# Forgetting attention: VectorE normalises the preceding unit's rows ahead of the maximum of this slot's scores

## The chip, the cores and the metric

The kernel runs on one core of one Trainium2 chip. The core has a matrix engine (TensorE, PE in the rows below, with its weight loads as PEld), VectorE (DVE), ScalarE (ACT), GpSimd (POOL), and SyncE (SP), which here only starts DMAs. Each engine takes its instructions strictly in its own program order, and they meet only at semaphores. The metric is device time in microseconds (us) of one execution.

## The reference

The reference is a trunk of two layers over a stream of 512 tokens of width 1024, in float32. Layer 0 has a mixer of a gated recurrence and differential attention, layer 1 has forgetting attention; each is followed by a residual LayerNorm and by a SwiGLU block (2816 wide) with another LayerNorm. The part that matters here is the attention of layer 1, with 16 heads of width 64:

```python
s = einsum('bhqd,bhkd->bhqk', qb, k) * scale + (cb[..., :, None] - c[..., None, :])
mask = k_pos[None, :] <= q_pos[:, None]
p = jax.nn.softmax(jnp.where(mask, s, MASK_VALUE), axis=-1)
return jnp.einsum('bhqk,bhkd->bhqd', p, v)
```

q and k are projections of the stream, each head's row scaled by the inverse root of its mean square; c is the running sum of the log forget gates. The output is multiplied with sigmoid(g) and goes through an output projection.

## The kernel before

**Products.** Every large product is split in three (high by low, low by high, high by high halves of float32), so TensorE carries three matmuls for each one of the reference. The weights come in 107 chunks through a ring: DMA to `w_raw`, ScalarE rounds to `w_hi` (L1036, 1.9 us for a whole chunk), GpSimd takes the rest to `w_lo` (L996, four instructions in a row), TensorE consumes.

**Slots.** In layer 1 the projections and the attention are interleaved by one list, `fox_steps`, which every engine walks. A step has a quarter of a weight chunk (a "piece") or a "slot" number s, or both. There are 32 units of attention, each a pair of heads (8) by a tile of 128 queries (4); unit u has keys 0 to (u mod 4 + 1) x 128, so its tiles are 128, 256, 384 and 512 wide in turn. In slot s

- TensorE does the piece, then turns a finished tile of q or k (`turn_heads`, L849, to bank 3), then the scores of unit s (L863 to L871, two banks out of 5, 6, 7), then transposes the probabilities of unit s-2 (`turn_pair`, L879, banks 3 and 4), then multiplies those of unit s-3 with v (L897, bank 2);
- ScalarE, after the work on the piece of the step before, takes the two exponentials of unit s with their row sums (L1286), then copies one transposed map of unit s-2 (L1229);
- VectorE, after the work on the pieces before, takes the row maxima of unit s (in one instruction, L1621, where its banks lie side by side, else in two, L1624 and L1625), normalises the maps of unit s-1 (a reciprocal, L1632, and two multiplications, L1635), copies the other transposed map of unit s-2 (L1644), and evacuates an output of unit s-3 where one is due.

**The path of q and k.** A piece of q or k goes round the engines: ScalarE copies it to `q_raw` and squares it to `sq` (L1058, L1254); VectorE sums the squares and adds epsilon (L1566, L1567); ScalarE takes logarithm and exponential (L1053, L1054); VectorE refines the root (L1332 to L1335) and scales the rows (L1577, `qn`); TensorE turns them into bank 3; ScalarE copies them to `qk` (L1263). Bank 3 is also the first bank of `turn_pair`, so TensorE's L879 waits for that copy. These pieces lie at the slots 0 to 4, 8 to 12 and 16 to 20; elsewhere the pieces are of v or of the gate and need none of this.

**Waits around the change.** `chain(ins, sem)` lets the engine go on only when the instruction is done. `full(key)` waits for a bank that TensorE has filled. `fmax` (VectorE to ScalarE) releases the exponentials, `fexp` (ScalarE to VectorE) says that unit u's exponentials are done, `fnorm` (VectorE to TensorE) releases `turn_pair`. The maximum of slot s >= 4 already waits for `fexp` of unit s-4; the normalisation of unit s-1 waits for `fexp` of unit s-1.

Of the kernel before, what the change touches and what calls it, by code (L numbers as in the profile page):

```python
# [35 lines left out]
ALU = mybir.AluOpType  # L36
# [3 lines left out]
P = 128  # L40
D = 1024
TS = 512
NT = TS // P
# [83 lines left out]
def build(nc, w, out):  # L127
# [5 lines left out]
    with ExitStack() as ctx:  # L133
# [6 lines left out]
        def place(name, free, dt, size):  # L140
            t = at(name, [P, *free], dt, top[0])
            n = size
            for f in free:
                n *= f
            top[0] += -(-n // 32) * 32
            return t
# [15 lines left out]
        small = place("small", [48], F32, 4)  # L162
# [4 lines left out]
        def take(name, free, dt, at_el):  # L167
            t = at(name, [P, *free], dt, arena + 4 * at_el)
            n = 1
            for f in free:  # L170
                n *= f
            return t, at_el + n
# [40 lines left out]
        p_fox, e = take("p_fox", [3, 2, TS], F32, e)  # L213
# [16 lines left out]
        def sem(name):  # L230
            return ctx.enter_context(nc.semaphore(name))
# [10 lines left out]
        act_step, dve_step = sem("act_step"), sem("dve_step")  # L242
        T_hi, T_lo = sem("T_hi"), sem("T_lo")
        S = {}
# [73 lines left out]
        n = 0  # L318
# [23 lines left out]
        F_UNITS = PAIRS * NT  # L342
# [12 lines left out]
        def heads_at(i):  # L355

            if not 0 <= i < len(fox_steps) or fox_steps[i][0] is None:
                return None
            c, p = fox_steps[i][0]
            stage = chunks[c][0]  # L360
            if stage[3] not in "qk":
                return None
            part, j = "qk".index(stage[3]), int(stage[4])
            return part, j, p, (2 * j + part) * NT + p
# [635 lines left out]
        def reader_of(eng, counts):  # L1000
            def full(key):
                bank, n, _ = uses[key]
                eng.wait_ge(bank_full[bank], n)
                return psum[bank]

            def chain(ins, s):

                ins.then_inc(s, 1)
                counts[id(s)] = counts.get(id(s), 0) + 1
                eng.wait_ge(s, counts[id(s)])  # L1010

            return full, chain
# [291 lines left out]
        def _(dve):  # L1304
            counts = {}
            full, chain = reader_of(dve, counts)
            step = lambda ins: chain(ins, dve_step)
            release = lambda ins, key: chain(ins, freed["dve"][uses[key][0]])
            v = nc.vector
            tt, ts, stt = v.tensor_tensor, v.tensor_scalar, v.scalar_tensor_tensor  # L1310
# [151 lines left out]
            for s in range(N + 4 + ROOT_LAG):  # L1462
# [3 lines left out]
                u = s - 4  # L1466
# [8 lines left out]
                if s < N:  # L1475
                    n = (s % NT + 1) * P
# [4 lines left out]
                    c, b = 24 + 4 * (s % 2), uses[("score", s, 0)][0]  # L1481
                    chain(v.tensor_reduce(small[:, c:c + 2], banks[:, b:b + 2, 0:n], AX_X, ALU.max, negate=True),  # L1482
                          S["max_done"])
                if 1 <= s <= N:

                    u = s - 1
                    n = (u % NT + 1) * P
                    c = 26 + 4 * (u % 2)
# [6 lines left out]
                u = s - 4 - ROOT_LAG  # L1495
# [67 lines left out]
            def square_sums(part, j, t, n):  # L1563
                dve.wait_ge(S["sq_done"], n + 1)
                m = fox_ms[:, n % 2, :, :]
                step(v.tensor_reduce(m[:, 0, :], sq[:, n % 2, :].rearrange("p (h d) -> p h d", h=4), AX_X, ALU.add))  # L1566
                chain(ts(m[:, 0, :], m[:, 0, :], 1.0 / HD, 1e-6, ALU.mult, ALU.add), S["qvar"])  # L1567

            def fox_heads(part, j, t, n):

                m = fox_ms[:, n % 2, :, :]
                dve.wait_ge(S["qroot"], n + 1)
                refine(m[:, 1, :], m[:, 0, :], m[:, 2, :])
                if n >= 2:

                    full(("heads", n - 2))
                chain(tt(qn[:, n % 2, :].rearrange("p (h d) -> p h d", h=4),  # L1577
                         q_raw[:, n % 2, :].rearrange("p (h d) -> p h d", h=4),
                         m[:, 1, :].unsqueeze(2).to_broadcast([P, 4, HD]), ALU.mult), S["qn_done"])
# [13 lines left out]
            for i, (piece, s) in enumerate(fox_steps):  # L1593
                if i == 2:
                    z, e = gate_T[0:FH, 0, :], gate_T[0:FH, 1, :]
                    release(ts(z, full("fox_f")[0:FH, :], gains[0:FH, 6:7], None, ALU.add), "fox_f")
                    chain(stt(e, z, -1.0, z, ALU.mult, ALU.min), S["f_arg"])
                    step(ts(z, z, 0.0, None, ALU.min))
                    dve.wait_ge(S["f_ln"], 1)
                    step(v.tensor_tensor_scan(z, z, e, 0.0, ALU.add, ALU.subtract))  # L1600

                    parts = [c_parts[0:FH, k, :] for k in range(3)]
                    step(ts(parts[0], z, -1.0, None, ALU.mult))
                    step(stt(z, z, -1.0, parts[0], ALU.mult, ALU.subtract))
                    step(v.tensor_copy(parts[1], z))
                    step(tt(z, z, parts[1], ALU.subtract))
                    chain(v.tensor_copy(parts[2], z), S["c_split"])
                if heads_at(i - 2):
                    fox_heads(*heads_at(i - 2))
                if heads_at(i - 1):  # L1610
                    square_sums(*heads_at(i - 1))
                if s is not None and s < F_UNITS:
                    n = (s % NT + 1) * P
                    c = 2 * (s % 4)
                    if s >= 4:
                        dve.wait_ge(S["fexp"], s - 3)
                    for m in range(2):
                        full(("fs", s, m))
                    a, b = SCORE_BANKS[s % 3]
                    if b - a == 1:  # L1620
                        ins = v.tensor_reduce(small[:, 16 + c:18 + c], banks[:, a:b + 1, 0:n], AX_X, ALU.max,  # L1621
                                              negate=True)
                    else:
                        step(v.tensor_reduce(small[:, 16 + c:17 + c], psum[a][:, 0:n], AX_X, ALU.max, negate=True))  # L1624
                        ins = v.tensor_reduce(small[:, 17 + c:18 + c], psum[b][:, 0:n], AX_X, ALU.max, negate=True)  # L1625
                    chain(ins, S["fmax"])
                if s is not None and 1 <= s <= F_UNITS:

                    u = s - 1
                    n, c = (u % NT + 1) * P, 2 * (u % 4)  # L1630
                    dve.wait_ge(S["fexp"], u + 1)
                    step(v.reciprocal(small[:, 32 + c:34 + c], small[:, 24 + c:26 + c]))  # L1632
                    for m in range(2):
                        p = p_fox[:, u % 3, m, 0:n]
                        ins = ts(p, p, small[:, 32 + c + m:33 + c + m], None, ALU.mult)  # L1635
                        chain(ins, S["fnorm"] if m else dve_step)
                if s is not None and 2 <= s < F_UNITS + 2:

                    u = s - 2
                    n = (u % NT + 1) * P  # L1640
                    acc = full(("fT", u, 1))
                    if u >= 2:
                        full(("fv", u - 2))
                    release(v.tensor_copy(pT_fox[:, u % 2, 1, 0:n], acc[:, 0:n]), ("fT", u, 1))  # L1644
                    dve.sem_inc(S["fpT_b"], 1)
                if s is not None and s >= 3:
                    u = s - 3
                    pair, t = u // NT, u % NT
                    acc = full(("fv", u))
                    if pair == PAIRS - 1:  # L1650
                        tok = slice(t * P, (t + 1) * P)
                        release(out_gate(pair, acc[:, tok], tok), ("fv", u))
                        dve.sem_inc(S["o_gated"], 1)
                        if t == 0:
                            out_lo(4)
                            out_lo(5)
                            out_lo(PAIRS - 2)
                        out_lo(pair, tok, t)
                    elif t == NT - 1 and pair == PAIRS - 2:
                        release(out_gate(pair, acc[:, :]), ("fv", u))  # L1660
                        dve.sem_inc(S["o_gated"], 1)
                    elif t == NT - 1:
                        release(v.tensor_copy(oT[:, pair, :], acc[:, :]), ("fv", u))
                f = gate_at(i - 1)
                if f is not None and f <= 5:
                    chain(out_gate(f, oT[:, f, :]), S["o_gated"])
                if f == 2:
                    out_lo(0)
                if f is not None and 2 <= f <= 4:
                    out_lo(f - 1)  # L1670
# [57 lines left out]
```

## Time and profile before

| | us |
|---|---|
| median of 3 runs (lowest, highest) | 1447.54 (1446.81, 1448.47) |
| the profiled execution's own time | 1443.57 |
| its span, first to last instruction | 1441.4 |
| TensorE busy in the span | 1363.5 (95%) |
| VectorE, ScalarE, GpSimd busy | 504.0, 492.8, 528.6 |
| mean granted TensorE clock | 0.981 |

The layer's attention, slots 0 to 31, lies between 774 us and 1030 us of the span. A row of the timeline has the start in us from the span's start, the duration in us, engine, line, operation, what is written and read, and in square brackets how long the engine had been idle before it and what ended that.

### The profile page before, as it was taken

The page shows a single profiled execution, that of the slowest core. Times are in us where ns is not written, and L with a number is a line of the kernel's source. Part 1 is how long each engine was busy: PE and PEld are TensorE (multiplying, and loading weights), DVE is VectorE, ACT ScalarE, POOL GpSimd, SP SyncE. Part 2 cuts the span into 40 slices and gives each one's busy share as a digit, 9 for nine tenths or more (in the row PEclk, how much of TensorE's full clock was granted, in tenths as well). Part 3 has the DMA queues.
Part 4 walks back from the last instruction along what each step waited for, and adds up shares of the span by engine and source line. Part 5 has one row for each costly group of instructions (what it writes and reads, how often), then busy time and mean ns, then how long its engine had stood idle before and what let it go on. Part 6 is the DMA issues. An engine that isn't in the chain of part 4 may idle for free.

```text
span 1441.4 us, 19076 instructions
## 1 busy us (share of the span) xinstructions
PE 1363.5 (95%) x7304; PEld 1132.6 (79%) x7304; DVE 504.0 (35%) x1054; ACT 492.8 (34%) x830; POOL 528.6 (37%) x421
## 2 busy tenths in 40 slices
PE   7999997789999999999988999899999999999997
PEld 7888874568888888887877778767788888888876
DVE  3366435655111111011653565654471111110005
ACT  4312326433223223211354554554333232232120
POOL 5421322042544543643333221222234445445350
PEclk9999998899999999999989999999999999999999
DMA  6311121022233232333133112202122332333231
GB/s 222 100 52 59 59 88 30 30 88 60 88 110 95 88 103 88 102 102 104 60 88 88 52 39 59 59 30 85 63 88 88 97 108 88 92 99 117 74 116 59
DMA packets 140137, 119.56 MB, mean 83 GB/s; under 512 B 5600, under 2 KB 118416, under 8 KB 140048
## 3 DMA queue, kind: packets, MB, share of 16 engines
q1 hardware_dynamic: 140048, 118.36, 26.5%
q8 instruction: 58, 0.95, 0.3%
q14 instruction: 31, 0.25, 0.1%
HBM read 116.20 MB, written 2.10 MB: 82 GB/s over the span
## 4 chain that ended last, share of the span: by engine, by line
PE 78%; DVE 9%; ACT 6%; issue 4%; POOL 2%; DMA 0%; ACTq 0%; DVEq 0%; POOLq 0%; SPq 0%
PE banks L471 24%; PE banks L473 23%; PE banks L472 23%; ACT w_hi L1036 2%; POOL w_lo L996 2%; PE banks L750 1%; PE banks L863 1%; PE banks L897 1%; PE banks L879 1%; DVE fox_ms L1567 1%; PE banks L817 1%; PE banks L768 1%; DVE small L1482 1%; DVE fox_ms L1566 1%; DVE o_even L1448 1%
## 5 line engine op out<-in xcount | busy, mean ns | idle before, releaser
L996 POOL TENSOR_TENSOR w_lo<-w_raw,w_hi 128x512 fp32r<-128x512 f32 x417 | 528.4, 1300 | 876.6 <-ACT w_hi L1036 847.5
L471 PE MATMUL banks<-xT_lo,w_hi 128*128 128x512 f32 (+2 forms) x992 | 371.9, 375 | 2.6 <-DVEq L1328 2.6
L473 PE MATMUL banks<-xT_hi,w_hi 128*128 128x512 f32 (+2 forms) x992 | 368.7, 372 | 0.0
L472 PE MATMUL banks<-xT_hi,w_lo 128*128 128x512 f32 (+2 forms) x992 | 368.6, 372 | 0.0
L1036 ACT ACTIVATE w_hi<-w_raw 128x2048 fp32r<-128x2048 f32 (+1 forms) x107 | 200.0, 1870 | 186.2 <-PE banks L473 143.6
L471 PEld LDWEIGHTS banks<-xT_lo,w_hi 128*128 128x128 f32 (+1 forms) x992 | 186.4, 188 | 36.3 <-issue 4.9
L473 PEld LDWEIGHTS banks<-xT_hi,w_hi 128*128 128x128 f32 (+1 forms) x992 | 186.5, 188 | 32.6
L472 PEld LDWEIGHTS banks<-xT_hi,w_lo 128*128 128x128 f32 (+1 forms) x992 | 186.6, 188 | 31.5
L471 PE MATMUL banks<-w_lo,xT_hi 128*128 128x256 f32 (+1 forms) x544 | 187.8, 345 | 15.5 <-ACT q_raw L1058 10.0
L472 PE MATMUL banks<-w_hi,xT_lo 128*128 128x256 f32 (+1 forms) x544 | 181.5, 334 | 0.0
L473 PE MATMUL banks<-w_hi,xT_hi 128*128 128x256 f32 (+1 forms) x544 | 181.5, 334 | 0.0
L1546 DVE TENSOR_TENSOR banks<-silu_g,banks 128x512 f32<-128x512 f32 x44 | 30.6, 696 | 402.7 <-PE banks L473 402.7
L471 PE MATMUL banks<-w_lo,hT_hi 128*128 128x512 f32 x352 | 137.3, 390 | 3.6 <-POOL w_lo L996 3.6
L473 PE MATMUL banks<-w_hi,hT_hi 128*128 128x512 f32 x352 | 137.0, 389 | 0.0
L472 PE MATMUL banks<-w_hi,hT_lo 128*128 128x512 f32 x352 | 136.9, 389 | 0.0
L1201 ACT ACTIVATE silu_g<-banks 128x512 f32<-128x512 f32 x44 | 26.4, 599 | 306.9 <-PE banks L473 306.9
L471 PEld LDWEIGHTS banks<-w_lo,xT_hi 128*128 128x128 f32 x544 | 106.9, 197 | 29.9 <-ACT q_raw L1058 11.0
L473 PEld LDWEIGHTS banks<-w_hi,xT_hi 128*128 128x128 f32 x544 | 107.0, 197 | 9.2
L472 PEld LDWEIGHTS banks<-w_hi,xT_lo 128*128 128x128 f32 x544 | 107.2, 197 | 8.1
L1507 DVE SCALAR_TENSOR_TENSOR x_res<-x_res,banks 128x512 f32<-128x512 f32 x32 | 22.0, 688 | 219.5 <-PE banks L473 218.8
L471 PEld LDWEIGHTS banks<-w_lo,hT_hi 128*128 128x128 f32 x352 | 66.1, 188 | 18.0 <-issue 4.4
L473 PEld LDWEIGHTS banks<-w_hi,hT_hi 128*128 128x128 f32 x352 | 66.1, 188 | 13.8
(178 smaller groups left out, 1229.8 us busy)
## 6 DMA issues: line engine op xcount, KB each, us to landing
w_raw<-in_ffn_w_dram SPq DMA_DIRECT2D x92, 512.0 KB, 4.1
w_raw<-in_ffn_w_dram SPq DMA_DIRECT2D x20, 1024.0 KB, 5.0
w_raw<-in_fox_w_in_dram SPq DMA_DIRECT2D x16, 1024.0 KB, 5.9
w_raw<-in_even_w_in_dram SPq DMA_DIRECT2D x14, 1024.0 KB, 5.0
w_raw<-in_even_w_out_dram SPq DMA_DIRECT2D x4, 1024.0 KB, 5.0
w_raw<-in_fox_w_out_dram SPq DMA_DIRECT2D x4, 1024.0 KB, 4.9
x_res<-in_x_dram SPq DMA_DIRECT2D x4, 512.0 KB, 7.7
out_dram<-x_res SPq DMA_DIRECT2D x4, 512.0 KB, 2.6
```

Of the source, the lines that this page charges most:

```text
L471: mm(acc, l_hi, r_lo, start=first, stop=False)
L472: mm(acc, l_lo, r_hi, start=False, stop=False)
L473: return mm(acc, l_hi, r_hi, start=False, stop=final)
L750: ins = mm(halves(acc[:, tok], z)[:, :, 1, :], k[:, tok], halves(q[:, tok], z)[:, :, 1, :], start=True, stop=True)
L768: ins = mm(acc[:, t * P:(t + 1) * P], scT[:, h % 2, PAIR[(s, t)], :], iv[:, s, h * P:(h + 1) * P], start=s == 0, stop=s == t)
L817: mm(acc[:, 0:n], bqT[rows, h, i * P:(i + 1) * P], bkT[rows, h, 0:n], start=True, stop=False)
L863: mm(acc[:, 0:n], qk[rows, j % 2, 0, pair % 2, i * P:(i + 1) * P], qk[rows, j % 2, 1, pair % 2, 0:n], start=True, stop=False)
L996: ins = nc.gpsimd.tensor_tensor(w_lo[c % RING][:, a:a + n], w_raw[c % RAW][:, a:a + n], w_hi[c % RING][:, a:a + n].bitcast(F32), ALU.subtract)
L1036: chain(fn(w_hi[c % RING][:, 0:size], w_raw[c % RAW][:, 0:size], ACT.Copy), hi_ready)
L1201: release(fn(silu_buf(j), acc[:, :], ACT.Silu), (f"up{l}", j, 0))
L1507: release(stt(xs, xs, ALPHA, full(key)[:, :], ALU.mult, ALU.add), key)
L1546: release(tt(h_buf(j), silu_buf(j), acc[:, :], ALU.mult), (f"up{l}", j, 1))
```

## The change

On VectorE, and only there, the block that normalises unit s-1 (with its wait for `fexp`) is moved from behind the maximum of unit s to ahead of it. In the program after the change the normalisation is at L1612 to L1621 and the maximum at L1622 to L1636.

```diff
                 if heads_at(i - 1):
                     square_sums(*heads_at(i - 1))
+                if s is not None and 1 <= s <= F_UNITS:
+
+                    u = s - 1
+                    n, c = (u % NT + 1) * P, 2 * (u % 4)
+                    dve.wait_ge(S["fexp"], u + 1)
+                    step(v.reciprocal(small[:, 32 + c:34 + c], small[:, 24 + c:26 + c]))
+                    for m in range(2):
+                        p = p_fox[:, u % 3, m, 0:n]
+                        ins = ts(p, p, small[:, 32 + c + m:33 + c + m], None, ALU.mult)
+                        chain(ins, S["fnorm"] if m else dve_step)
                 if s is not None and s < F_UNITS:
                     n = (s % NT + 1) * P
                     c = 2 * (s % 4)
...
                     chain(ins, S["fmax"])
-                if s is not None and 1 <= s <= F_UNITS:
-
-                    u = s - 1
-                    n, c = (u % NT + 1) * P, 2 * (u % 4)
-                    dve.wait_ge(S["fexp"], u + 1)
-                    step(v.reciprocal(small[:, 32 + c:34 + c], small[:, 24 + c:26 + c]))
-                    for m in range(2):
-                        p = p_fox[:, u % 3, m, 0:n]
-                        ins = ts(p, p, small[:, 32 + c + m:33 + c + m], None, ALU.mult)
-                        chain(ins, S["fnorm"] if m else dve_step)
                 if s is not None and 2 <= s < F_UNITS + 2:
```

VectorE's rows at slot 3, before (`fox_ms` holds the sums and roots of q or k, `small` the maxima, row sums and reciprocals, `p_fox` the maps, `banks` PSUM):

```order
L1566 TENSOR_REDUCE fox_ms<-sq 128x4
L1567 TENSOR_SCALAR fox_ms<-fox_ms 128x4
L1621 TENSOR_REDUCE small<-banks 128x2
L1632 RECIPROCAL small<-small 128x2
L1635 TENSOR_SCALAR p_fox<-p_fox,small 128x384 x2
L1644 COPY pT_fox<-banks 128x256
L1332 TENSOR_TENSOR fox_ms<-fox_ms 128x4
```

VectorE's rows at the same place after the change:

```order
L1566 TENSOR_REDUCE fox_ms<-sq 128x4
L1567 TENSOR_SCALAR fox_ms<-fox_ms 128x4
L1617 RECIPROCAL small<-small 128x2
L1620 TENSOR_SCALAR p_fox<-p_fox,small 128x384 x2
L1631 TENSOR_REDUCE small<-banks 128x2
L1644 COPY pT_fox<-banks 128x256
```

The reciprocal and the two multiplications of unit 2 have passed the maximum of unit 3; what follows the three stays where it was. The same holds in slot 31, here as the difference, VectorE again:

```order
-L1624 TENSOR_REDUCE small<-banks 128x1
-L1625 TENSOR_REDUCE small<-banks 128x1
-L1632 RECIPROCAL small<-small 128x2
-L1635 TENSOR_SCALAR p_fox<-p_fox,small 128x384 x2
+L1617 RECIPROCAL small<-small 128x2
+L1620 TENSOR_SCALAR p_fox<-p_fox,small 128x384 x2
+L1634 TENSOR_REDUCE small<-banks 128x1
+L1635 TENSOR_REDUCE small<-banks 128x1
 L1644 COPY pT_fox<-banks 128x256
```

Nothing else moves on VectorE, and the order on TensorE, ScalarE, GpSimd and SyncE is the same in both programs.

## Rows read from the trace of the kernel before

**Rows 1.** Waits of TensorE in 773 to 1030 us: total, times, longest.
```profile
PE banks L879 <- ACT qk L1263: 10.4, 8, 2.3
```

**Rows 2.** Timeline of VectorE, slots 1 to 3.
```profile
784.53 0.42 DVE L1624 TENSOR_REDUCE small<-banks 128x1 f32<-128x256 f32 x1
...
785.45 0.17 DVE L1632 RECIPROCAL small<-small 128x2 f32<-128x2 f32 x1
785.65 0.61 DVE L1635 TENSOR_SCALAR p_fox<-p_fox,small 128x128 f32<-128x128 f32 x2
...
788.43 0.96 DVE L1621 TENSOR_REDUCE small<-banks 128x2 f32<-128x768 f32 x1
...
789.63 0.75 DVE L1635 TENSOR_SCALAR p_fox<-p_fox,small 128x256 f32<-128x256 f32 x2
...
798.88 1.23 DVE L1621 TENSOR_REDUCE small<-banks 128x2 f32<-128x1024 f32 x1
...
800.34 1.60 DVE L1635 TENSOR_SCALAR p_fox<-p_fox,small 128x384 f32<-128x384 f32 x2
...
803.87 0.42 DVE L1566 TENSOR_REDUCE fox_ms<-sq 128x4 f32<-128x256 f32 x1
```

**Rows 3.** Timeline of ScalarE, slots 2 and 3.
```profile
789.61 0.58 ACT L1286 ACTIVATE p_fox<-banks,small 128x384 f32<-128x384 f32 x1 [0.17 <-ACT qk L1263]
...
800.14 0.69 ACT L1286 ACTIVATE p_fox<-banks,small 128x512 f32<-128x512 f32 x1 [0.25 <-DVE small L1621]
...
802.82 0.42 ACT L1254 ACTIVATE sq<-q_raw 128x256 f32<-128x256 f32 x1
```

**Rows 4.** Timeline of TensorE, its waits in slots 3 and 4.
```profile
800.03 0.63 PE L879 MATMUL banks<-ident,p_fox 128*128 128x128 f32 x4 [2.26 <-ACT qk L1263]
...
805.69 0.85 PE L879 MATMUL banks<-ident,p_fox 128*128 128x128 f32 x6 [0.56 <-ACT qk L1263]
```

**Rows 5.** Timeline of GpSimd, two of its bursts.
```profile
796.34 4.93 POOL L996 TENSOR_TENSOR w_lo<-w_raw,w_hi 128x512 fp32r<-128x512 f32 x4 [13.37 <-ACT w_hi L1036]
...
858.73 4.93 POOL L996 TENSOR_TENSOR w_lo<-w_raw,w_hi 128x512 fp32r<-128x512 f32 x4 [14.80 <-PE banks L473]
```

**Rows 6.** Timeline of VectorE, slots 6, 8 to 11, 17 and 18.
```profile
822.22 2.52 DVE L1635 TENSOR_SCALAR p_fox<-p_fox,small 128x256 f32<-128x256 f32 x2
...
834.70 0.42 DVE L1621 TENSOR_REDUCE small<-banks 128x2 f32<-128x256 f32 x1 [1.68 <-PE banks L871]
...
845.50 0.69 DVE L1621 TENSOR_REDUCE small<-banks 128x2 f32<-128x512 f32 x1
...
850.24 0.56 DVE L1624 TENSOR_REDUCE small<-banks 128x1 f32<-128x384 f32 x1 [0.31 <-PE banks L871]
...
861.28 1.23 DVE L1621 TENSOR_REDUCE small<-banks 128x2 f32<-128x1024 f32 x1
...
909.05 0.69 DVE L1621 TENSOR_REDUCE small<-banks 128x2 f32<-128x512 f32 x1
...
917.27 0.96 DVE L1621 TENSOR_REDUCE small<-banks 128x2 f32<-128x768 f32 x1 [1.01 <-PE banks L871]
```

**Rows 7.** Timeline of ScalarE, slots 7, 11 and 19.
```profile
832.29 0.69 ACT L1286 ACTIVATE p_fox<-banks,small 128x512 f32<-128x512 f32 x1
...
868.31 0.47 ACT L1263 ACTIVATE qk<-banks,gains 128x256 f32<-128x256 f32 x1 [0.89 <-PE banks L849]
...
935.85 0.47 ACT L1263 ACTIVATE qk<-banks,gains 128x256 f32<-128x256 f32 x1 [1.16 <-PE banks L849]
```

**Rows 8.** Timeline of TensorE: slots 11 and 19, and the last unit.
```profile
862.43 0.63 PE L879 MATMUL banks<-ident,p_fox 128*128 128x128 f32 x4 [1.90 <-ACT qk L1263]
...
929.98 0.63 PE L879 MATMUL banks<-ident,p_fox 128*128 128x128 f32 x4 [1.96 <-ACT qk L1263]
...
1028.40 1.09 PE L897 MATMUL banks<-pT_fox,v_all 128*64 128x128 f32 x16 [0.75 <-DVE oT L1584]
```

**Rows 9.** Stages: us, busy times, granted clock, DMA share, GB/s.
```profile
930.00:935.00 5.00, 5.00 (x30) 4.66 (x31) 3.51 (x14) 3.16 (x9) 0.00 (x0) 0.67 0.46 153
```

## The prediction, made before the changed kernel was run

> **What bounds the kernel now.** I read the page first: TensorE is busy 95% of the span, so a change on VectorE can cost or bring only what it adds to or takes from TensorE's waits. The reader then looks at the waits of TensorE within the attention of layer 1. They are few: eight of its transposes of the probabilities (L879) wait 10.4 us in all for ScalarE's copy to `qk` [rows 1]. These waits lie where pieces of q and k go round the engines beside the slots: slots 1 to 4, 8 to 11, 16 to 20. In all other slots TensorE does not wait, and VectorE has time. Third, the timeline of VectorE, for one question in each slot: was the engine idle before the maximum? Seven times of 32 it was not: slots 1, 2, 3, 9, 11, 17 and 19. In slots 1 to 3 the scores lie ready and the maximum starts as soon as VectorE is free [rows 2]. Elsewhere it waited for the scores, for 0.31 us in slot 10, 1.01 in slot 18, 1.68 in slot 8 [rows 6] and mostly for longer.
>
> **What is moved and its size.** 32 normalisations are moved, of which 31 pass a maximum. Each is a reciprocal and two multiplications. The 128-wide one takes 0.84 us: 785.45 to 785.65 for the reciprocal, 0.61 for the pair, 0.03 for the hand-over. The 256-wide takes 0.20 + 0.75 + 0.04 = 0.99. The 384-wide took 0.20 + 1.60 + 0.04 = 1.84 in slot 3 [rows 2]. Undisturbed the widths suggest 1.12: between 128 and 256 columns the pair grew by 0.14, so 0.75 + 0.14 = 0.89, and 0.23 around it. For 512 the same step gives 1.25. Nothing is added or removed, and no DMA or queue is passed. The work on other engines stays in order, so only dates change.
>
> **Where VectorE was idle: nothing or a small gain.** With an idle time longer than the normalisation, it fits in ahead of the maximum and the maximum keeps its date. The copy behind it comes earlier by as much. TensorE does not wait for that copy or for `fnorm` in any slot (no such wait stands among those of rows 1), so the gain has no taker. One small taker may be at the end: the last product with v waited 0.75 us for VectorE's output step [rows 8]. That step follows the copy of the last unit's transposed map, which cannot start before TensorE has turned it, so I credit 0.1 to 0.2 of the 0.75.
>
> **Where VectorE was not idle: the maximum is late, and the exponentials, and all behind them on ScalarE.** Those are the q and k steps on which TensorE waits.
>
> Stretch one, slots 1 to 4. In slot 1 the maximum is 0.84 late. In slot 2 another 0.99 is put before it. Before, the exponentials of slot 2 did not start at the end of the maximum (788.43 + 0.96 = 789.39, some 0.09 to the other engine) but at 789.61, behind a `qk` copy [rows 3], so 0.13 is absorbed: 0.84 + 0.99 - 0.13 = 1.70. This goes through `q_raw`, `sq`, the sums, the root and the `qk` copy, at each of which the next engine was waiting, to the L879 at 800.03, where TensorE already waits [rows 4]: 1.70 us later. In slot 3 the 384-wide normalisation comes before the maximum. GpSimd's burst for the next chunk (796.34, four instructions in 4.93 us [rows 5]) moves with ScalarE's rounding, so by 1.70 too, to 798.0 to 803.0. The normalisation now starts at 798.88 + 1.70 = 800.6, at the same place in the burst at which the maximum used to stand, and no longer at its end. What a pair of multiplications costs inside a burst is in slot 6: 2.52 us for the 256-wide pair that took 0.75 otherwise [rows 2, 6], as if each multiplication had to wait for the instruction of GpSimd under way (4.93 / 4 = 1.23 us). Here the burst ends after 2.4 us, so I take 2.5 for the whole normalisation; bounds 1.12 (undisturbed) and 2.7. The exponentials of slot 3 are then 1.70 + 2.5 = 4.2 late. On the way to the next wait there is slack: `sq` was done at 802.82 + 0.42 = 803.24 [rows 3], VectorE summed it at 803.87 [rows 2], so 0.63 - 0.1 = 0.53 is absorbed. TensorE's L879 at 805.69 [rows 4] is 4.2 - 0.5 = **3.7 us** later (2.3 undisturbed, 3.9 at most). Behind it TensorE is busy without a wait until the next stretch, so nothing of it is given back.
>
> The Trainium skill (SBUF — State Buffer, section "Who interferes with whom") says that VectorE and GpSimd share one pair of ports as an exclusive lock, which an instruction holds to its end while the other is blocked. It speaks against this change: the maximum reads PSUM and is not subject to the lock, the multiplications on SBUF are, and the change lets them take the maximum's place within the burst. The trace agrees with it at 822.22 (2.52 us). By a sharing of bandwidth in its place the 384-wide normalisation would stay near the 1.84 us of its row, and stretch one would come to 3.0 us.
>
> Stretch two, slots 9 to 11. Slot 9: 0.84. Slot 10: 0.99 less the idle 0.31, so 1.5; about 0.45 goes into the slack before the sum as above, and the L879 at 862.43 is 1.1 later [rows 8]. Slot 11: the 384-wide normalisation again falls inside a burst (858.73 + 1.1 to 863.66 + 1.1; it starts at 861.28 + 1.1 = 862.4 [rows 5, 6]): 2.6, so 3.7 for the exponentials, less 0.45 of slack, less the 0.89 that the next `qk` copy had waited for TensorE [rows 7]. That leaves **2.3 us** (1.1 undisturbed).
>
> Stretch three, slots 17 to 20. Slot 17: 0.84, through to the L879 at 929.98 [rows 8]. Slot 18: the idle 1.01 takes the 0.99. Slot 19: 1.12 more, outside a burst, and the next `qk` copy had waited 1.16 for TensorE [rows 7], so it is absorbed. **0.8 us**.
>
> Sum: 3.7 + 2.3 + 0.8 - 0.1 = 6.7 us. Against the profiled execution's own 1443.57 that is 1450.3; the median of the runs is 1447.54, some 4 us above that execution, and I put the same 6.7 on it: **1454.2 us**.
>
> **The added wait.** The maximum of slot s now stands behind the exponentials of unit s-1. The tightest place is slot 8: those of slot 7 end at 832.29 + 0.69 and about 0.2 for the row sum, the 512-wide normalisation then needs 1.25 and ends at 834.4, the scores are ready for the maximum at 834.70 [rows 6, 7]. It fits by some 0.3 us. If it did not, slots 8, 16 and 24 would cost a few tenths each, under 1 us.
>
> **Rivals.**
> - Only part arrives. The bursts do not hit the moved multiplications (the undisturbed bounds: 2.3 + 1.1 + 0.8 - 0.1 = 4.1, so 1451.6). For it: the burst's phase is an argument of mine from 1.7 us of shift. Against it: 1.60 us in slot 3 was already disturbed.
> - Nearly nothing arrives. Only the first delay of each stretch counts, since later ones overlap with TensorE's own waits: 3 x 0.84 = 2.5, so 1450.0. For it: 95% busy TensorE and short queues. Against it: in slots 2 and 3 the waiting engine is each time the next on the path.
> - Clock. TensorE's granted clock was 0.67 in the 5 us behind the wait at 929.98 [rows 8, 9], that is at the lower of its two levels (1.2 GHz) for two thirds of them; this costs 0.33 x 5 = 1.65 us where TensorE is the bound. Longer waits could bring two more such stretches: 6.7 + 3.3, so 1457.5.
> - Faster. The mechanism is the earlier copy and the earlier q and k work behind the maximum, in the slots where VectorE idles. It decides if the sum L1566 there starts when VectorE comes free and not when `sq` is done. If each of four of the eight L879 waits [rows 1] became shorter by 0.99, this would give -4, so 1443.5. Against it: behind the idle slots VectorE again waits for `sq`, and at slots 1 to 3 it is never idle, where the order alone can win nothing.
> - That the change does not do what it says is excluded by the order of the instructions.
>
> **How the numbers follow.** Forecast 0.40, bursts missed 0.25, clock 0.12, nearly nothing 0.17, faster 0.06. What a measurement of this kernel can tell from no change is about 0.2%, 2.9 us, so 1444.6 to 1450.4 is "same". Slower: 0.40 + 0.25 + 0.12 = 0.77; same 0.17; faster 0.06. The range goes from 1448.5, below the "nearly nothing" case, to 1458.5, above the clock case. Left out are the faster case and the tails.
>
> **What would show it.** In the profile after: TensorE's waits for the `qk` copy in the attention grow from 10.4 to some 17 us; the maxima of slots 1, 2 and 3 start 0.84, 1.8 and 4.2 us later against the start of slot 0; the pair of 384-wide multiplications in slots 3 and 11 takes 2 us or more; the pair in slot 6, moved ahead of its burst, falls to 0.75; from slot 21 on, the distances are unchanged. Wrong: a maximum late by 4 us in slot 3 with L879 on its old date, or VectorE's idle time before the maxima giving way to a wait for the exponentials.

## The result, and the profile after

| | before | after |
|---|---|---|
| median of the runs compared (lowest, highest), 4 each | 1448.01 (1446.81, 1451.13) | 1459.20 (1458.21, 1460.39) |
| ratio, 95% interval | | 1.0074 (1.0056 to 1.0093) |
| the profiled execution: own time, span | 1443.57, 1441.4 | 1460.39, 1458.3 |
| mean granted clock in it | 0.981 | 0.972 |

The kernel became slower by 0.74%, which is 10.7 us of 1448 (the two medians are 11.2 apart). The direction was as forecast, the size was not: 1454.2 had been forecast, and 1459.2 lies 0.7 above the end of the range. The page after, busy times of the engines:

```profile
PE 1374.2 (94%) x7304; PEld 1141.0 (78%) x7304; DVE 502.6 (34%) x1054; ACT 492.8 (34%) x830; POOL 529.0 (36%) x421
```

VectorE, ScalarE and GpSimd are as busy as before to 1.4 us. Only TensorE, with the same instructions, is busy 10.7 us longer (1363.5 before). The two spans differ by 16.9 us. Of these 5.2 are there before slot 0 begins, where both programs are the same (in the traces below slot 0 begins anywhere between 773.7 and 781.6 us), 10.5 come between the scores of slot 0 and those of slot 31, and 1.1 after. So I compare the stage from slot 0 to slot 31: before, then after (span, busy times of the five engines, granted clock, DMA share, GB/s).

```profile
774.40:1017.90 243.50, 228.67 (x1682) 182.78 (x1680) 139.37 (x346) 127.02 (x308) 59.92 (x48) 0.99 0.18 53
```
```profile
779.60:1033.60 254.00, 234.09 (x1681) 187.00 (x1680) 138.99 (x349) 127.02 (x308) 60.17 (x48) 0.96 0.17 51
```

10.5 us = 5.4 of TensorE busy and 5.1 of TensorE idle (14.8 to 19.9). The busy part is clock: by the granted clock, not rounded, TensorE was at the lower of its two levels for 6.8 us of the stage before and for 20.5 us after (the rounded 0.99 and 0.96 give 2 x 0.01 x 243 = 4.9 and 2 x 0.04 x 254 = 20.3). The idle part by cause, TensorE's waits in 778 to 1045 us after (total, times, longest), to hold against [rows 1]:

```profile
PE banks L879 <- ACT qk L1263: 9.8, 8, 1.8
PE banks L879 <- DVE p_fox L1620: 2.0, 1, 2.0
PE banks L863 <- ACT p_fox L1286: 2.0, 1, 2.0
PE banks L849 <- DVE qn L1577: 1.9, 2, 0.9
PE banks L849 <- ACT pT_fox L1229: 1.0, 1, 1.0
```

The waits for `qk` did not grow to 17: 9.8, and 11.8 with the row named `p_fox` L1620. That row is a `qk` wait under another name: the matmul starts at 944.49, the `qk` copy before it ended at 944.34 and the multiplication at 944.42, and the wait is put down to the last. What is new is L849, the turning of q and k, which before waited only once for 0.2 us, and 0.9 more at L863. Two of its three waits in the timeline of TensorE:

```profile
812.80 0.41 PE L849 MATMUL banks<-ident,qn 128*128 128x128 f32 x2 [1.03 <-ACT pT_fox L1229]
...
859.10 0.41 PE L849 MATMUL banks<-ident,qn 128*128 128x128 f32 x2 [0.95 <-DVE qn L1577]
```

L849 writes bank 3. Bank 3 must be free of unit s-3's transposed map, which ScalarE copies out (L1229) behind the exponentials, and these are late. The copy that frees bank 3 for the second of the two rows, on ScalarE:

```profile
858.35 0.60 ACT L1229 ACTIVATE pT_fox<-banks 128x512 f32<-128x512 f32 x1 [0.17 <-ACT p_fox L1286]
```

858.35 + 0.60 = 858.95, and 0.15 later L849 starts. The two others of its three waits ended 0.15 behind such a copy too (812.65 to 812.80, 926.25 to 926.40), and so did the start in the trace of before (848.20 to 848.35, with 0.07 of idle time there). The profile names `qn`, but the `qn` that it means is the next tile's; the tile turned here lay ready since 854.70. The late work reached TensorE through this bank too, not only through `qk`.

VectorE after, slots 2 and 3, to hold against [rows 2]:

```profile
789.97 0.61 DVE L1620 TENSOR_SCALAR p_fox<-p_fox,small 128x128 f32<-128x128 f32 x2
790.61 0.42 DVE L1634 TENSOR_REDUCE small<-banks 128x1 f32<-128x256 f32 x1
...
795.49 0.96 DVE L1631 TENSOR_REDUCE small<-banks 128x2 f32<-128x768 f32 x1
...
804.89 0.42 DVE L1566 TENSOR_REDUCE fox_ms<-sq 128x4 f32<-128x256 f32 x1 [3.04 <-ACT sq L1254]
805.35 1.17 DVE L1567 TENSOR_SCALAR fox_ms<-fox_ms 128x4 f32<-128x4 f32 x1
806.55 0.17 DVE L1617 RECIPROCAL small<-small 128x2 f32<-128x2 f32 x1
806.75 2.52 DVE L1620 TENSOR_SCALAR p_fox<-p_fox,small 128x384 f32<-128x384 f32 x2
809.31 1.23 DVE L1631 TENSOR_REDUCE small<-banks 128x2 f32<-128x1024 f32 x1
```

Slot 0 begins 5.22 us later than before. Measured from it, the maxima of slots 1, 2 and 3 are late by 790.61 - 784.53 - 5.22 = 0.86, by 795.49 - 788.43 - 5.22 = 1.84 and by 809.31 - 798.88 - 5.22 = 5.21. The first two are the forecast 0.84 and 1.8. The third was forecast at 4.2. The pair inside GpSimd's burst took 2.52, as in slot 6 before, and again in slot 11 (873.61, 2.52). The burst in slot 3:

```profile
804.00 5.06 POOL L996 TENSOR_TENSOR w_lo<-w_raw,w_hi 128x512 fp32r<-128x512 f32 x4 [15.81 <-ACT w_hi L1036]
```

The 5.21 divide into 2.44 by which L1566 is late (804.89 - 797.23 - 5.22; forecast 1.70) and 2.77 by which the maximum stands further behind it (4.42 us in place of 1.65; forecast 2.5). The 0.74 too much in the first goes with the clock: at 795 to 800 us TensorE was at its lower level, a stretch that the kernel before did not have, and in e6 below, without it, the shift at slot 3 is 4.42 = 1.65 + 2.77. Two of these windows after, in the first and third stretch of waits (columns as above):

```profile
795.00:800.00 5.00, 4.34 (x21) 4.37 (x22) 3.34 (x11) 2.91 (x9) 0.00 (x0) 0.50 0.00 0
945.00:950.00 5.00, 5.00 (x25) 4.34 (x24) 2.93 (x10) 2.87 (x8) 0.00 (x0) 0.50 0.36 123
```

The pair of slot 6 is ahead of its burst and fell to 0.74, and the tight place at slot 8 fitted: the maximum still waited 0.27 us for the scores, where 0.3 had been worked out.

```profile
827.79 0.74 DVE L1620 TENSOR_SCALAR p_fox<-p_fox,small 128x256 f32<-128x256 f32 x2
...
843.29 1.01 DVE L1620 TENSOR_SCALAR p_fox<-p_fox,small 128x512 f32<-128x512 f32 x2
844.57 0.42 DVE L1631 TENSOR_REDUCE small<-banks 128x2 f32<-128x256 f32 x1 [0.27 <-PE banks L871]
```

### The profile page after: what moved, and what is told of

It reads as the page before. It is cut to its first block, busy times and chain, and to the rows that moved or that the text cites. A ratio compares the mean times of both kernels' runs of the same rounds, so it can differ in the third digit from the quotient of the medians.

```text
span 1458.3 us, 19076 instructions
## 1 busy us (share of the span) xinstructions
PE 1374.2 (94%) x7304; PEld 1141.0 (78%) x7304; DVE 502.6 (34%) x1054; ACT 492.8 (34%) x830; POOL 529.0 (36%) x421
## 4 chain that ended last, share of the span: by engine, by line
PE 78%; DVE 9%; ACT 6%; issue 4%; POOL 2%; DMA 0%; ACTq 0%; DVEq 0%; POOLq 0%; SPq 0%
PE banks L471 24%; PE banks L473 23%; PE banks L472 23%; POOL w_lo L996 2%; ACT w_hi L1036 2%; PE banks L750 1%; PE banks L897 1%; PE banks L879 1%; PE banks L863 1%; DVE fox_ms L1567 1%; DVE fox_ms L1566 1%; DVE small L1482 1%; PE banks L768 1%; DVE p_fox L1620 1%; PE banks L817 1%
## 5 line engine op out<-in xcount | busy, mean ns | idle before, releaser
L471 PE MATMUL banks<-xT_lo,w_hi 128*128 128x512 f32 (+2 forms) x992 | 372.2, 375 | 2.0 <-DVEq L1328 1.6
L471 PEld LDWEIGHTS banks<-xT_lo,w_hi 128*128 128x128 f32 (+1 forms) x992 | 186.8, 188 | 35.9 <-issue 4.5
L471 PE MATMUL banks<-w_lo,xT_hi 128*128 128x256 f32 (+1 forms) x544 | 189.9, 349 | 15.2 <-ACT q_raw L1058 10.1
L471 PE MATMUL banks<-w_lo,hT_hi 128*128 128x512 f32 x352 | 138.7, 394 | 3.6 <-POOL w_lo L996 3.6
L471 PEld LDWEIGHTS banks<-w_lo,xT_hi 128*128 128x128 f32 x544 | 108.8, 200 | 30.1 <-ACT q_raw L1058 11.0
L471 PEld LDWEIGHTS banks<-w_lo,hT_hi 128*128 128x128 f32 x352 | 66.8, 190 | 18.2 <-issue 4.4
L472 PEld LDWEIGHTS banks<-w_hi,hT_lo 128*128 128x128 f32 x352 | 67.0, 190 | 13.9
```

Of the source, the lines that this page charges most:

```text
L471: mm(acc, l_hi, r_lo, start=first, stop=False)
L472: mm(acc, l_lo, r_hi, start=False, stop=False)
```

## The experiments

The measure within a trace is the shift: how much later than in the trace of before the maximum of a slot starts, both counted from the maximum of slot 0. It leaves out what happens before the attention. All are from one profiled execution each. The ratio compares whole runs, at least 6 of each kernel but for the 4 of the kernel after; 0.0010 of it is 1.4 us. It differs from the difference of the two medians by up to 1.5 us (e1).

| kernel | slot 1 | 2 | 3 | 5 | 8 | 13 | 16 | 31 | ratio to before (95%) |
|---|---|---|---|---|---|---|---|---|---|
| after | 0.86 | 1.84 | 5.21 | 4.67 | 4.65 | 8.36 | 8.36 | 10.53 | 1.0074 (1.0056, 1.0093) |
| e1, idle slots only | 0.01 | 0.02 | 0.02 | 0.84 | 0.84 | 0.01 | 0.01 | 0.07 | 1.0003 (0.9992, 1.0015) |
| e2, nine busy slots only | 0.86 | 1.84 | 4.59 | 5.53 | 5.52 | 8.08 | 8.08 | 8.93 | 1.0077 (1.0061, 1.0093) |
| e3, slots 1 to 3 only | 0.86 | 1.84 | 4.89 | 5.86 | 5.85 | 5.86 | 5.86 | 4.73 | 1.0049 (1.0032, 1.0067) |
| e4, slots 3 and 11 only | 0.02 | 0.02 | 2.78 | 2.25 | 2.25 | 3.70 | 3.69 | 3.68 | 1.0026 (1.0014, 1.0039) |
| e5, before, bank 4 first | 0.00 | 0.00 | 0.00 | -0.39 | -0.39 | -0.73 | -0.86 | -2.39 | 0.9967 (0.9955, 0.9978) |
| e6, after, bank 4 first, filled | 0.86 | 1.83 | 4.42 | 3.48 | 3.49 | 5.65 | 5.52 | 5.98 | 1.0033 (1.0017, 1.0048) |
| e7, before, bank 4 first, filled | 0.00 | 0.00 | 0.02 | -0.38 | -0.38 | -1.60 | -1.74 | -3.31 | 0.9973 (0.9960, 0.9985) |
| e8, e4 and fine bursts | -0.02 | -0.03 | 1.43 | 0.90 | 0.88 | 0.13 | 0.10 | 1.14 | 0.9989 (0.9973, 1.0005) |
| e9, before, fine bursts | -0.03 | -0.03 | 0.20 | 0.23 | 0.23 | -1.05 | -1.06 | -1.20 | 0.9977 (0.9966, 0.9988) |
| e10, before, bank 4 first, fine | -0.03 | -0.03 | 0.26 | -0.10 | -0.10 | -2.02 | -2.15 | -2.90 | 0.9954 (0.9940, 0.9969) |
| e11, after, fine bursts | 0.82 | 1.80 | 3.43 | 4.37 | 4.36 | 6.18 | 6.16 | 8.09 | 1.0030 (1.0016, 1.0045) |
| e12, after, bank 4 first | 0.84 | 1.81 | 4.40 | 3.45 | 3.46 | 6.45 | 6.32 | 6.83 | 1.0039 (1.0023, 1.0054) |

### Where the loss arises: idle slots against busy slots

**e1.** The order after, except in the nine slots of the three stretches; `normalise` is the moved block.

```diff
+                early = s not in (1, 2, 3, 9, 10, 11, 17, 18, 19)
+                if early and s is not None and 1 <= s <= F_UNITS:
+                    normalise(s)
...
+                if not early and s is not None and 1 <= s <= F_UNITS:
+                    normalise(s)
```

> The normalisation goes ahead of the maximum only in the 22 slots (and behind the last) in which VectorE had idled before the maximum; slots 1 to 3, 9 to 11 and 17 to 19 keep the old order. Theory 'late maxima' (the cost arises only where VectorE had no idle time, because the exponentials and with them the q and k work come late): no change, 0 to -0.5 us against the kernel before. Rival 'added wait' (each moved normalisation costs a little, because the maximum now stands behind the exponentials of the unit before): 23 of 32 moves kept, so about +8 of the +11 us.

Measured: 1446.98 against 1448.10, ratio 1.0003. Moving 22 of the 31 costs and brings nothing that the time of whole runs can show. The added wait for the exponentials costs nothing.

**e2.** The complement.

```diff
+                early = s in (1, 2, 3, 9, 10, 11, 17, 18, 19)
```

> The other way round: the new order only in slots 1 to 3, 9 to 11 and 17 to 19. Theory 'late maxima': the whole loss, +10 to +11.5 us against the kernel before. Rival 'added wait': 9 of 32 moves, about +3 us.

Measured: 1458.72, ratio 1.0077, the whole loss. Nine of 31 moves carry it, seven of them in slots without idle time; slots 10 and 18 had 0.31 and 1.01 us.

**e3.** The first stretch alone.

```diff
+                early = s in (1, 2, 3)
```

> The new order only in slots 1, 2 and 3. 'Late maxima' by the order alone: +3.7 us; the changed kernel's trace has +4.65 from slot 0 to slot 5, the difference being one low-clock stretch in slots 2 and 3, so with the clock +4.5 to +5. Rival 'nothing is given in part' (each stretch is absorbed by TensorE's next wait for q and k, and only all together cost): under +1.5 us.

Measured: 1454.25, ratio 1.0049, 7.1 us (the medians are 6.2 apart), more than the 4.5 to 5 that I had expected. The shift is 4.89 at slot 3 and 5.86 at slot 5. The last step, 0.97 where e4 falls by 0.53, comes with a low-clock stretch between slots 4 and 5, where TensorE does not wait. At slot 31 the shift is 4.73, since the low-clock stretch that before had from 931.7 on is missing. So slots 1 to 3 give roughly half or more of the loss.

### The pair of multiplications inside a burst

**e4.** Only the two slots in which the 384-wide normalisation takes the maximum's place within a burst.

```diff
+                early = s in (3, 11)
```

> The new order only in slots 3 and 11, where the 384-wide normalisation falls into a burst of GpSimd. If each multiplication waits for the instruction of GpSimd under way: pair of 2.2 to 2.5 us, exponentials 2.7 late, +2.1 in slot 3 and about +1.3 in slot 11, +3.4 us in all, with a low-clock stretch more +5. If the multiplications only share bandwidth (pair of about 1.6 us as before): 1.84 late less 0.5 of slack in slot 3 and nothing in slot 11 because the copy to qk had waited 0.9 for TensorE, so +1.3 to +1.8 us.

Measured: 1451.61, ratio 1.0026, 3.8 us (the medians are 3.5 apart), as expected; slot 5 late by 2.25, and 1.45 more at slot 13. VectorE in slot 3:

```profile
806.16 0.17 DVE L1618 RECIPROCAL small<-small 128x2 f32<-128x2 f32 x1
806.36 2.52 DVE L1621 TENSOR_SCALAR p_fox<-p_fox,small 128x384 f32<-128x384 f32 x2
```

**e8.** As e4, and GpSimd's instructions for the layer's input projections half as long and twice as many. If each multiplication waits for the instruction under way, the pair gets shorter; if the two share bandwidth, the same bytes cost the same.

```diff
-                for a in range(0, size, 512):
-                    n = min(512, size - a)
+                w = 256 if chunks[c][0].startswith("fox") else 512
+                for a in range(0, size, w):
+                    n = min(w, size - a)
```

> The new order only in slots 3 and 11, and GpSimd's instructions for the weights of this layer's input projection are 256 columns wide instead of 512, so each is about half as long and a burst has eight. If a multiplication of VectorE waits for GpSimd's instruction under way: the pair in slots 3 and 11 falls from 2.52 us to 1.3 to 1.8, and the loss of 3.7 us of the same order with 512-wide instructions falls to +1.5 to +2.5. If the two share bandwidth: pair at 2.5 us as before, loss unchanged.

Measured: 1447.90, ratio 0.9989: no loss is left, where 1.5 to 2.5 had been expected, since the fine bursts bring something by themselves (e9). The same pair, the burst that it falls into, and GpSimd's groups (busy us, mean ns):

```profile
801.66 1.36 DVE L1622 TENSOR_SCALAR p_fox<-p_fox,small 128x384 f32<-128x384 f32 x2
```
```profile
799.90 5.79 POOL L997 TENSOR_TENSOR w_lo<-w_raw,w_hi 128x256 fp32r<-128x256 f32 x8 [13.62 <-ACT w_hi L1037]
```
```profile
L997 POOL TENSOR_TENSOR w_lo<-w_raw,w_hi 128x512 fp32r<-128x512 f32 x352 | 447.4, 1303 | 659.1 <-ACT w_hi L1037 659.1
L997 POOL TENSOR_TENSOR w_lo<-w_raw,w_hi 128x256 fp32r<-128x256 f32 x128 | 90.6, 745 | 210.2 <-ACT w_hi L1037 182.3 <-PE banks L473 27.9
```

2.52 became 1.36 in both slots (864.07 too), while GpSimd's work on the same bytes got longer (2 x 745 ns in place of 1303). Outside a burst the 384-wide pair takes 0.88 (slot 19 of the kernel after, 943.54), so 1.64 of waiting became 0.48. The wait goes with the length of the neighbour's instruction, not with its bytes. The Trainium skill (SBUF — State Buffer, "Who interferes with whom") calls this an exclusive lock held to an instruction's end; this pair of traces agrees.

**e9.** The kernel before with that edit alone.

> The kernel before with GpSimd's instructions for this layer's input projection 256 columns wide. VectorE's instructions that waited 1.2 us inside a burst (among them the small ones at L1567 and L1332) should wait half as long; some of these lie on the q and k path: -1 to -3 us against the kernel before. If the fine instructions cost more (GpSimd 0.75 us each instead of half of 1.30, a burst 0.9 us longer) and a chunk comes late: 0 to +1.

Measured: 1443.36 against 1447.30, ratio 0.9977, a little more than expected. Against it, e8's order costs 0.67 at slot 5 (0.90 - 0.23) in place of 2.25: most of the price of slot 3 was the lock.

**e11.** The kernel after with it.

> The changed kernel with fine bursts. With the new order only in slots 3 and 11 the fine bursts took 2.5 us by the stage and 3.7 by the medians. The same in the full change: +6.5 to +8.5 us against the kernel before in place of +11. If the collision with the bursts did not matter in the full change: +10 to +11.

Measured: 1451.17, ratio 1.0030, so 8.0 us under the kernel after, and less than the 6.5 to 8.5 above the kernel before that I had expected. But e9 gained from the same edit, and against e9's 1443.36 the order still costs 7.8: fine bursts take away part of the price (2.9 of 10.7), not its root. In the traces it is less: the shift at slot 31 is 8.09 + 1.20 = 9.3 against e9, in place of 10.5.

### Clock and bank

**e5.** The kernel before, in which `turn_pair` turns the map of bank 4 first, so that the wait for bank 3 stands behind useful work.

```diff
-                for m in range(2):
+                for m in (1, 0):
...
-                        full(("fT", s - 3, 1))
+                        full(("fT", s - 3, 0))
```

> The kernel before, but TensorE transposes the map of the second head (bank 4) ahead of that of the first (bank 3), so that less of its work stands behind the wait for the copy to qk. The three stretches are latency chains through ScalarE and VectorE, so only the last wait of each stretch should shrink, by the 0.3 to 0.8 us of the transposes moved ahead: -0.5 to -2 us against the kernel before. If the waits add up one by one on TensorE instead: eight times 0.2 to 0.8, -3 to -4 us.

Measured: 1444.22 against 1448.83, ratio 0.9967. More in the median than I expected; in the trace 2.4, of which 1.8 arise in slots 19 to 20, where the low-clock stretch of before is missing.

**e6.** The kernel after with the same edit, and the first transposes repeated where TensorE would wait, so that it keeps working (the repeats write the same values).

```diff
+                    again = (6, 6, 2, 1)[u % NT] if m and u in (0, 1, 2, 8, 9, 10, 16, 17, 18) else 1
+                    for j in list(range(u % NT + 1)) * again:
```

> The changed kernel with bank 4 first, and in the slots of the q and k work the transposes into bank 4 are repeated (6, 6 or 2 times for 128, 256 or 384 keys; the same values are written again), so that TensorE works through much of its waits. Theory 'late maxima plus clock': the order costs about 7 of the 11 us and the rest is low granted clock called forth by the longer waits; with the waits filled the low-clock time between slots 0 and 31 falls from 20 us to under 7 and the kernel is at +5 to +7.5 us against the kernel before (the gain of bank 4 first is in that). Rival 'all is order': the clock changes or not, the time stays at +9 to +11.

Measured: 1452.59, ratio 1.0033, 4.8 us. That is just under the 5 to 7.5 of the theory, but it doesn't show that the order costs only 7: bank 4 first brought 4.8 us by itself in e5, more than I had taken for it. What the order costs follows from e7 below.

**e7.** The kernel before with both edits.

> The kernel before with the same two edits. Theory: bank 4 first brings 0.5 to 2 us and the filled waits up to the 3 us that its two low-clock stretches cost, so -1 to -4 us against the kernel before. If the fillers only lengthen TensorE's work where it does not wait long enough: 0 to +2 us.

Measured: 1444.91, ratio 0.9973. **e12**, the kernel after with bank 4 first and no repeats:

> The changed kernel with bank 4 first and no repeated transposes: the control of the run with filled waits (+3.3 per mille, +4.8 us). If the fillers did their part through the clock, this one lies between it and the changed kernel: +6 to +9 us, with a mean clock of 0.972 to 0.977 where the filled one has 0.981 to 0.984. If bank 4 first alone did it: +4.5 to +5.5 with the same clock as the filled one.

Measured: 1452.67 against 1447.30, ratio 1.0039, 5.6 us, with a mean clock of 0.977: the clock as I had expected it without the repeats, the time nearly that of e6. In the profiled executions of e6 and e7 the stage has no low-clock time at all:

```profile
776.30:1025.80 249.50, 232.48 (x1736) 185.34 (x1734) 139.23 (x349) 126.91 (x308) 60.11 (x48) 1.00 0.17 52
```
```profile
777.60:1017.90 240.30, 231.66 (x1736) 185.28 (x1734) 139.84 (x346) 126.88 (x308) 59.95 (x48) 1.00 0.18 54
```

So the difference of these two is the order alone, in kernels that both have bank 4 first and the repeats. It is 5.98 + 3.31 = **9.3 us** at slot 31: 3.86 by slot 5, 3.4 between 8 and 13 (2.16 against -1.22), 2.0 between 16 and 31 (0.46 against -1.57). e12 less e5 gives 9.2. Whole runs give 9.0 as the difference of the means of all 12 runs of e6 and e7, 7.7 as that of the medians. Where the clock is the same they agree better: runs of e6 with a mean clock of 0.983 or 0.984 took 1450.67 (mean of 4), those of e7 1441.64 (mean of 4), 9.0 apart; before and after at 0.974 to 0.976 took 1449.5 (10 runs) and 1459.1 (2 runs), 9.6 apart. The rest of the 10.7, some 1 to 2 us, is left for the clock: 0.974 in the mean of the runs after, 0.978 of before. It is a remainder and was not measured by itself.

Against a larger part of the clock speak e6 and e12: the repeats raised the mean clock from 0.977 to 0.981, and the time stayed (1.0033 and 1.0039, intervals overlap). The repeats take TensorE's time too, so this does not exclude a small part. In e1 to e4 the number and the place of the low-clock stretches differ from execution to execution, so one trace can't say how many the order brings.

**e10.** The kernel before with bank 4 first and fine bursts.

> The kernel before with bank 4 first and fine bursts. If the two gains are independent, the gain of bank 4 first (0.33%, 4.7 us) and that of the fine bursts (1 to 3 us) add: -5.5 to -7.5 us. If both mostly ease the same granted clock, they overlap: -4 to -5 us.

Measured: 1440.87 against 1447.30, ratio 0.9954: the best version, 6.4 us under the kernel before. That lies in the first branch: by the ratios it is 6.7, where the two edits alone give 4.8 and 3.3.

## Why the prediction was wrong in size

**Where it costs: right.** Only the three stretches in which VectorE had no or little idle time before the maximum count (e1 nothing, e2 all). "Faster" and "nearly nothing" fall with that, and so does a price of the added wait.

**Stretch one, 3.7: right.** 3.86 without low-clock time. The dates of slots 1 and 2 were met to 0.04, and the whole normalisation in the burst cost 2.77 where 2.5 (at most 2.7) had been taken. "Only part arrives" falls: the bursts did hit both pairs.

**Stretch two, 2.3, and stretch three, 0.8: the step that failed.** They measured 3.4 and 2.0. I had subtracted 0.89 and 1.16 because the next `qk` copy had waited that long for TensorE [rows 7], and took these waits for slack. They were made by the clock of that one execution. Before the first of them TensorE was at its lower level for two thirds of 5 us, and so it was before the second [rows 9]:

```profile
863.00:868.00 5.00, 5.00 (x31) 4.80 (x30) 3.40 (x10) 2.69 (x9) 0.67 (x1) 0.66 0.62 179
```

TensorE came late to L849, and ScalarE waited. In e7 the clock stays up at both places, and the two copies (slots 11 and 19) have no wait:

```profile
870.33 0.47 ACT L1264 ACTIVATE qk<-banks,gains 128x256 f32<-128x256 f32 x1
...
936.21 0.47 ACT L1264 ACTIVATE qk<-banks,gains 128x256 f32<-128x256 f32 x1
```

e7 has two more edits. e1 has none that touches these slots, and its trace says the same. There TensorE was at its lower level in slot 3, not in slot 11, and again in slot 19; the copies of slots 3, 11 and 19:

```profile
807.38 0.47 ACT L1263 ACTIVATE qk<-banks,gains 128x256 f32<-128x256 f32 x1 [0.85 <-PE banks L849]
...
869.78 0.47 ACT L1263 ACTIVATE qk<-banks,gains 128x256 f32<-128x256 f32 x1
...
937.38 0.47 ACT L1263 ACTIVATE qk<-banks,gains 128x256 f32<-128x256 f32 x1 [1.12 <-PE banks L849]
```

Without the two subtractions my own steps give 3.7 - 0.5 = 3.2 and 0.84 + 1.12 = 2.0, and with 3.7 and -0.1 a sum of 8.8, so 1456.3. What is missing from there to the 10.7 is 0.5 of sizes and the 1 to 2 us left for the clock. Where both executions have low clock at these places, the subtraction does hold: e2, TensorE at its lower level near both, has 2.56 in stretch two and 0.85 in stretch three against the trace of before, close to my 2.3 and 0.8. But in that trace stretch one cost 5.53 in place of 3.86, with low clock in slots 2 and 4, and the sum was 8.9 all the same. So I had counted what the low clock gives (waits that absorb a delay) and not what it takes. I had used [rows 9] to price a rival and had not asked what the same low clock did to the rows beside it.

**Clock, priced at nothing in the forecast: too low.** The lower level went from 6.8 to 20.5 us of the profiled stage, and TensorE was busy 5.4 longer. Most of that lay beside work that was late anyway: of the 10.5 us only 1.2 remain above the 9.3 of the order. The rival (two more stretches, +3.3) had the direction; in the runs 1 to 2 are left for it. What makes a stretch come in one execution and not in the next stays open.

**Where TensorE waits: half right.** I had named `qk` as the only channel (17 us), although the trace of before has waits of 1.1 at L863 and 2.8 at L471 in the attention too (2.8 after). Bank 3, freed by a ScalarE copy behind the late exponentials, is another: 2.9 us at L849, and 0.9 more at L863, while `qk` took 11.8 in place of 10.4.

**The small gain at the end, 0.1: right.** TensorE's wait for `oT` lies behind the maximum of slot 31, so the shifts don't show it. It is 0.75 us before and 0.63 after, and it follows the order of the last slots in the other traces too: 0.63 in e1, 0.74 to 0.75 in e2, e3 and e4, 0.58 in e7 against 0.48 in e6. The size is as forecast, the times of whole runs can't show it.

## What to carry to other kernels

Before moving a producer ahead of another on a shared engine, find in each slot whether that engine was idle there. Where it was not, the move delays the other producer by its full length (0.84 and 0.98 in slots 1 and 2), however rarely that is; where no one waits for its result, it brings nothing. A wait that you mean to subtract as slack must be there in other executions too; look at the granted clock just before it, since a low-clock stretch of the upstream engine makes such waits. Put those instructions of VectorE that a burst of GpSimd delays (here multiplications on SBUF) outside the bursts, or make the burst's instructions shorter; and let a consumer with two banks begin with the one that isn't awaited.

## What the runs showed of the hardware

A burst also delays small instructions of VectorE on SBUF: L1567, on 128x4 elements, took 1.17 us in the burst of slot 3 after (above) and 0.17 outside it. It does not delay all of them: in the same burst the sum L1566 took 0.42 and the reciprocal 0.17, as they do outside, though both read and write SBUF. Nor did a maximum from PSUM get longer (1.23 at 798.88 before, inside the burst of [rows 5]). Splitting GpSimd's instruction in two raised its own time by 14% (2 x 745 against 1303 ns) and still made the kernel before faster (e9, 0.9977). The same program, the kernel before, took 1443.6 to 1451.9 us, and its time goes with the mean granted clock: 1445.1 at 0.982 (5 runs), 1445.6 at 0.980 (19), 1448.8 at 0.978 (24), 1449.6 at 0.976 (8). The runs grouped here are from three chips, and on each of the three the runs at 0.980 are faster than those at 0.978. That is as much as many a change is worth, so one profiled execution should not be held against one other without the clock of both.
